# RWKV recurrence output: the v and u products merged over 128 rows, k-r taken apart from k-a

## What is computed

```python
def rwkv7_step(S, inp):
    r, w, k, v, a, b = inp
    sa = jnp.einsum('dbhvk,dbhk->dbhv', S, a)
    S = S * w[..., None, :] + sa[..., None] * b[..., None, :] + v[..., :, None] * k[..., None, :]
    y = jnp.einsum('dbhvk,dbhk->dbhv', S, r)
    return S, y
```

## Time and profile before

| what | value |
| --- | --- |
| median of 3 runs | 3094.26 us (3088.29 to 3096.70) |
| profiled execution | 3099.59 us, its span 3097.8 us, mean granted clock 0.955 |
| PE | busy 2801.7 us, 90% of the span |
| PE weight loads | busy 2233.2 us, 72% |
| DVE | busy 2077.6 us, 67% |
| ACT | busy 1340.7 us, 43% |
| POOL | busy 745.1 us, 24% |

### The profile page before, as it was taken

One profiled execution on the slowest core, in us unless ns is written; L12 is line 12 of the kernel. 1 busy time (PEld: TensorE's weight loads), 2 busy tenths in 40 slices (PEclk: granted clock), 3 DMA queues, 4 the chain that ended last, 5 costly groups with the idle time before them and its releaser, 6 DMA issues. The chain is left out here.

```text
span 3097.8 us, 62311 instructions
## 1 busy us (share of the span) xinstructions
PE 2801.7 (90%) x24610; PEld 2233.2 (72%) x24610; DVE 2077.6 (67%) x3080; ACT 1340.7 (43%) x2582; POOL 745.1 (24%) x895
## 2 busy tenths in 40 slices
PE   7889989997747999997899789999799999799999
PEld 4565578884447998895666678888588888588887
DVE  5767623236756665543545878888888888588786
ACT  4547711114434554443334434444544444344443
POOL 4547700004636787741223100000000000000000
PEclk9999999998868999998999899999899999899999
DMA  4432223224784444333555232222122222636411
GB/s 129 143 92 50 50 79 73 70 54 138 298 246 147 139 143 138 107 109 124 163 181 181 79 123 83 81 82 82 55 81 80 79 80 73 249 118 211 162 36 55
DMA packets 302490, 361.25 MB, mean 117 GB/s; under 512 B 119977, under 2 KB 202409, under 8 KB 302082
## 3 DMA queue, kind: packets, MB, share of 16 engines
q1 hardware_dynamic: 297314, 352.01, 35.6%
q10 hardware_dynamic: 4896, 5.38, 0.5%
HBM read 254.16 MB, written 103.14 MB: 115 GB/s over the span
## 5 line engine op out<-in xcount | busy, mean ns | idle before, releaser
L99 PE MATMUL up_p<-up_b_hi,up_a_hi 128*128 128x512 f32 x1232 | 491.1, 399 | 43.3 <-ACT inv L2286 23.3
L100 PE MATMUL up_p<-up_b_lo,up_a_hi 128*128 128x512 f32 x1232 | 490.8, 398 | 0.0
L101 PE MATMUL up_p<-up_b_hi,up_a_lo 128*128 128x512 f32 x1232 | 490.1, 398 | 0.0
L99 PEld LDWEIGHTS up_p<-up_b_hi,up_a_hi 128*128 128x128 f32 x1232 | 234.0, 190 | 104.3 <-ACT inv L2286 25.0
L100 PEld LDWEIGHTS up_p<-up_b_lo,up_a_hi 128*128 128x128 f32 x1232 | 234.0, 190 | 56.0
L101 PEld LDWEIGHTS up_p<-up_b_hi,up_a_lo 128*128 128x128 f32 x1232 | 233.9, 190 | 55.6
L2729 ACT CAST down_a_hi<-down_a 128x512 fp32r<-128x512 f32 x154 | 96.0, 623 | 260.6 <-PE down_p_x L101 144.6
L2241 ACT CAST up_a_hi<-up_a_sum 128x512 fp32r<-128x512 f32 x132 | 81.3, 616 | 231.7 <-DVE up_a_sum L2400 151.4
L2744 DVE TENSOR_TENSOR down_a_lo<-down_a,down_a_hi 128x512 fp32r<-128x512 f32 x154 | 106.4, 691 | 98.5 <-ACT down_a_hi L2729 98.5
L2311 ACT ACTIVATE up_con<-up_raw,vecs_sb 128x1023 f32<-128x1023 f32 (+1 forms) x88 | 109.7, 1246 | 127.7 <-DVE up_raw L2470 84.2
L99 PE MATMUL down_p_x<-down_b_hi,down_a_hi 128*128 128x512 f32 x352 | 138.8, 394 | 20.0 <-DVE down_b_lo L2746 19.9
(11 more groups left out here) (298 smaller groups left out, 7449.7 us busy)
## 6 DMA issues: line engine op xcount, KB each, us to landing
up_a_raw<-in_w_up SPq DMA_DIRECT2D x172, 256.0 KB, 2.9
rec_inp<-gate_chunks SPq DMA_DIRECT2D x64, 512.0 KB, 3.6
down_a<-in_w_down SPq DMA_DIRECT2D x88, 256.0 KB, 8.6
down_b<-act_out SPq DMA_DIRECT2D x88, 256.0 KB, 8.8
first_w<-in_w_attn SPq DMA_DIRECT2D x24, 512.0 KB, 3.6
rkv_chunks<-rwkv_project_mix SPq DMA_DIRECT2D x12, 1024.0 KB, 6.5
gate_chunks<-gates_out SPq DMA_DIRECT2D x3, 4096.0 KB, 13.4
act_out<-up_con SPq DMA_DIRECT2D x22, 512.5 KB, 2.6
```

Source lines behind the costliest of these rows:

```text
L99: pe.matmul(out, w_hi, x_hi, start=start, stop=False, skip_group_check=True)
L100: pe.matmul(out, w_hi, x_lo, start=False, stop=False, skip_group_check=True)
L101: return pe.matmul(out, w_lo, x_hi, start=False, stop=stop, skip_group_check=True)
```

## The change

`akrk` (64 rows of a head: masked k-a beside masked k-r) becomes `ak` alone; `rb` becomes `rbrk`, which for each head h holds the masked b-r product in the head's own 64 rows and the masked k-r product in the other 64 rows, the same layout as `stacked`. The y stage then multiplies `stacked` by `rbrk` over all 128 rows, one matmul for each head in place of two. To bring k-r into the opposite half, it is taken out of `ak_part` into a stage of its own, `rk_part`, which writes the half opposite to the rows that it reads, as `tok_part` does. `rk_part` takes the place of `rb_part` in PE's list, and `rb_part` goes behind `h_part`, with a wait for `rk` of its direction. The ak mask covers 64 columns, the rb mask now covers rb and rk together.

```diff
@@ -1102,7 +1102,7 @@
                   "kept_odd",
                   "dec", "grow", "g_copied", "x_copied", "u_copied", "m_copied", "tok_copied", "v_copied", "y_copied",
                   "spread", "ar", "diag_a", "diag_b", "ak_masked", "rb_masked", "h_added", "h_decayed",
-                  "merged", "b", "k", "gram", "cross", "corner", "x", "u", "h", "ak", "rb", "tok_b", "tok", "y", "v"):
+                  "merged", "b", "k", "gram", "cross", "corner", "x", "u", "h", "ak", "rk", "rb", "tok_b", "tok", "y", "v"):
             S[n] = [ctx.enter_context(nc.semaphore(f"rec_{n}{d}")) for d in range(2)]
         G = {n: ctx.enter_context(nc.semaphore("rec_" + n)) for n in
              ("init", "dec_set", "mask_in", "turned", "solved", "returned", "step", "eye_zero", "eye_set", "first_quarter_in")}
@@ -1116,8 +1116,8 @@
         kt = sb("k", RING, RU, L)
         dec_end = sb("dec_end", NCH, RU)
         ring_g = sb("g", RING, RU, L)
-        akrk = sb("akrk", 2, RU, 2 * L)
-        rb = sb("rb", 2, RU, L)
+        ak = sb("ak", 2, RU, L)
+        rbrk = sb("rbrk", 2, RU, 2, L)
         toks = sb("toks", RU, 2, L)
         raw_v = lambda d, r: toks[d][:, :, r % 2]
         vtok = sb("vtok", 2, RU, L)
@@ -1305,7 +1305,7 @@
                     for u in range(RU):
                         if c > 0:
                             pair(to[:, u], ar[d][:, c % RING, u, 0:L], H[d][:, c % 2, u], True, False)
-                        mm = pair(to[:, u], akrk[d][:, c % 2, u, 0:L], vtok[d][:, c % 2, u], c == 0, True)
+                        mm = pair(to[:, u], ak[d][:, c % 2, u], vtok[d][:, c % 2, u], c == 0, True)
                     mm.then_inc(S["x"][d], 1)
 
                 def u_part(c, d):
@@ -1329,24 +1329,36 @@
                     done(pe, "u_copied", d, c + 1)
                     to = bank[d][1][:, :, 0:L]
                     for u in range(RU):
-                        pair(to[:, u], vtok[d][:, c % 2, u], akrk[d][:, c % 2, u, L:], True, False)
                         if c > 0:
-                            pair(to[:, u], H[d][:, c % 2, u], ar[d][:, c % RING, u, L:], False, False)
+                            pair(to[:, u], H[d][:, c % 2, u], ar[d][:, c % RING, u, L:], True, False)
                         for h, rows in enumerate(HALVES):
-                            mm = pe.matmul(to[rows, u], stacked[d][rows, c % 2, u, h], rb[d][rows, c % 2, u],
-                                           start=False, stop=True)
+                            mm = pe.matmul(to[rows, u], stacked[d][:, c % 2, u, h], rbrk[d][:, c % 2, u, h],
+                                           start=c == 0, stop=True)
                     mm.then_inc(S["y"][d], 1)
 
                 def ak_part(c, d):
                     done(pe, "ar", d, c + 1)
                     done(pe, "k", d, c + 1)
                     done(pe, "g_copied", d, min(NCH, c + LAG - 1))
-                    each(bank[d][2], kt[d][:, c % RING], ar[d][:, c % RING]).then_inc(S["ak"][d], 1)
+                    each(bank[d][2][:, :, 0:L], kt[d][:, c % RING], ar[d][:, c % RING, :, 0:L]).then_inc(S["ak"][d], 1)
+
+                def rk_part(c, d):
+                    done(pe, "ak_masked", d, c + 1)
+                    to = bank[d][2].rearrange("p u (j t) -> p u j t", j=2)
+                    for u in range(RU):
+                        for h, rows in enumerate(HALVES):
+                            mm = pe.matmul(to[HALVES[1 - h], u, h], kt[d][rows, c % RING, u],
+                                           ar[d][rows, c % RING, u, L:], start=True, stop=True)
+                    mm.then_inc(S["rk"][d], 1)
 
                 def rb_part(c, d):
-                    done(pe, "ak_masked", d, c + 1)
-                    each(bank[d][2][:, :, 0:L], bt[d][:, c % RING], ar[d][:, c % RING, :, L:]).then_inc(
-                        S["rb"][d], 1)
+                    done(pe, "rk", d, c + 1)
+                    to = bank[d][2].rearrange("p u (j t) -> p u j t", j=2)
+                    for u in range(RU):
+                        for h, rows in enumerate(HALVES):
+                            mm = pe.matmul(to[rows, u, h], bt[d][rows, c % RING, u], ar[d][rows, c % RING, u, L:],
+                                           start=True, stop=True)
+                    mm.then_inc(S["rb"][d], 1)
 
                 def tok_b_part(c, d):
                     done(pe, "v_copied", d, NCH // 2)
@@ -1405,7 +1417,8 @@
                 for c in SLOTS:
                     now, ahead, front = live(c), live(c + 1), live(c + LAG)
                     for go, stage, n in ((now, x_part, c), (ahead, ak_part, c + 1), (now, u_part, c),
-                                         (ahead, rb_part, c + 1), (now and c < NCH - 1, h_part, c),
+                                         (ahead, rk_part, c + 1), (now and c < NCH - 1, h_part, c),
+                                         (ahead, rb_part, c + 1),
                                          (now, y_part, c), (ahead, tok_b_part, c + 1), (ahead, tok_part, c + 1),
                                          (ahead, cross, c + 1), (front, gram, c + LAG),
                                          (ahead, corner, c + 1)):
@@ -1550,13 +1563,15 @@
                 def ak_mask(c, d):
                     done(dve, "ak", d, c + 1)
                     done(dve, "y", d, c - 1)
-                    tt(akrk[d][:, c % 2], bank[d][2][:, :, :], over_units(mask_of(f"both{d}")), ALU.mult).then_inc(
-                        S["ak_masked"][d], 1)
+                    tt(ak[d][:, c % 2], bank[d][2][:, :, 0:L], over_units(mask_of(f"both{d}")[:, 0:L]),
+                       ALU.mult).then_inc(S["ak_masked"][d], 1)
 
                 def rb_mask(c, d):
                     done(dve, "rb", d, c + 1)
                     done(dve, "y", d, c - 1)
-                    tt(rb[d][:, c % 2], bank[d][2][:, :, 0:L], over_units(mask_of(f"both{d}")[:, L:]),
+                    tt(rbrk[d][:, c % 2].rearrange("p u j t -> p (u j) t"),
+                       bank[d][2].rearrange("p u (j t) -> p (u j) t", j=2),
+                       mask_of(f"both{d}")[:, L:].unsqueeze(1).to_broadcast([P, 2 * RU, L]),
                        ALU.mult).then_inc(S["rb_masked"][d], 1)
 
                 def state(c, d):
```

## The result

The changed kernel takes 3129.99 us (median of 4 runs, 3127.40 to 3135.60) against 3095.48 us of the kernel before in the same comparison: ratio 1.0107, 95% interval 1.0086 to 1.0128. It is slower by 34.5 us, inside the range, with the sign of the forecast; the forecast itself had +50.

A forecast was written before the change was run, and what follows sets the result against it. The prediction took PE's own stream to bound the recurrence, about 15.1 us a slot. Its terms, 44.0 - 0.6 + 3.8 + 3, summed to +50 us, giving 3144 us, with a range of 3112 to 3168.

The forecast's parts named there:

- What bounds it: Recurrence, 960 to 1430 us: PE's own stream sets its length, about 15.1 us a slot; PE idle under issue 23.3 us.
- The y stage, +44.0 - 0.6: Y stage: eight groups fewer, 16 changes of shape at 0.147 us; +1.42 us a slot over 31 chunks, chunk 0 -0.6.
- the second rival: Y stage, half the cost: second pair's weight load runs ahead, 0.09 us a change stays; +22 us, 3116 us; chance 0.10.
- the first rival: Y stage: no cost for changes of shape in short groups; -14 us, 3080, with 8 given back at y copies; chance 0.09.
- k-a and k-r apart, +3.8: Ak and rk stages: 64 columns each in place of 128 together, +0.12 us a slot, x 32 = +3.8 us.
- The ak mask, +3: PE reaches rk 0.82 us earlier and waits for DVE's ak mask: 7 us at most, taken as +3 us.
- The order on DVE, 0: Rb mask before the state update on DVE: state, x and block transposes move later but stay covered; cost 0.
- Issue pauses unchanged: PE's issue pauses in the recurrence, 23.3 us: no term in the sum; range allowed 10 us less or more.
- the third rival: Recurrence: issue pauses grow with the waits, or the broken-up y stage lowers the clock, 45 us on top; 3190; chance 0.04.
- The sum: Whole kernel: 44.0 - 0.6 + 3.8 + 3 = +50 us, +1.6%, giving 3144 us.
- the full cost: Main case, every change of shape in the y stage costs 0.147 us: range 3128 to 3160, chance 0.77.

The follow-up runs named there:

- experiment 4: Kernel before, with its h stage taken unit by unit into the y stage: 434 more changes of shape, nothing merged; 3134.25 us, ratio 1.0084.
- 1: Changed kernel without the merged product: k-r apart but written to its own half, y again in three groups; 3139.04 us, ratio 1.0102 to the kernel before.
- 6: Kernel before, with the 128-column ak product taken as two of 64, 992 matmul instructions more; 3123.62 us, ratio 1.0072.
- 2: Changed kernel, y stage in two passes for each direction, all H products first, then the merged ones; 3117.98 us, ratio 1.0035 to the kernel before.
- 3: Changed kernel, H products as a stage of their own between k-r and b-r, y one merged pass; 3119.75 us, ratio 1.004 to the kernel before.
- the repeats: Kernel before and changed kernel, unedited, profiled once more: 3109.97 us (one execution) and 3141.07 us (ratio 1.0109).
- 7: Against the kernel before: merged, k-a and k-r kept together, b-r, u and b's tokens in the opposite half, H products separate; 3094.20 us, ratio 0.9976.
- 11: The fewer-products merged kernel, with DVE transposing the solved blocks ahead of the b-r masks; 3086.63 us, ratio 0.9934 to the kernel before.

## Why the prediction was right, and where it wasn't

- **What bounds it.** Right: the time before and behind the recurrence moved by 2 us at most in the profile, the recurrence by 30.9. "PE's own stream sets the length" was true, but I took "issue" for a fixed remainder of that stream, and it is a second bound with a rate of its own.
- **The y stage, +44.0 - 0.6.** Right. The groups stand 0.264 us apart (mean of 440) against 0.265, and 98% of the 544 changes take 148 to 152 ns from the last start to the next, in place of 51 or 52 inside a stage; the second pair starts 107 ns behind the first, in place of 58. So the 0.147 has the parts 0.10 and 0.05, where the prediction, rounding, read 0.09 and 0.05. y, tok_b and rb, whose borders these are, grew by 30.6 + 4.8 + 3.1 = 38.5 us between the two u starts; my sum for the 30 full slots and chunk 0 there is 30 x 1.42 - 0.6 = 42. The step that rested on a choice, that the price seen once after 32 instructions holds every four, was right; experiment 4 shows it without a merged product. (The Trainium skill, "TensorEngine Tiling", Key Properties, has the drain and no price; the measured one is 0.14 to 0.147 us.) The second pair behind a change is late in short groups as well, so half the cost, the second rival, is out, and so is the first, for the price itself; the 3116 us of the second rival are 14 us from the measured median, no farther than my 3144, so it is the trace and not the time that tells them apart.
- **k-a and k-r apart, +3.8.** Right for the stream: ak, rk and u together went from 82.6 to 86.2 us. Wrong as the price of the step: done alone (1) it costs 32 us, because there it brings 32 more instructions a slot, their blocks (6: 19 us in the time from the instructions alone), and waits. In the changed kernel the merge takes these 32 away again. So the sum held and two of its terms did not stand for themselves: 1 at +32 and the merge on top of it at about 0, where I had +7 and +43.
- **The ak mask, +3.** The right mechanism, mis-sized: waits for `rec_akrk` were 1.1 us, for `rec_ak` 6.8, +5.7 from start to start, inside my 0 to 7.
- **The order on DVE, 0.** Right: waits for the spread went from 2.6 to 2.3 us, and x doesn't wait for the state. It is a cover that the long y stage gives. Where y is short again (2, 3) the waits for the spread are 11.6 and 13.3 us, 9 and 11 more than before, the case that the first rival had put at 8.
- **Issue pauses unchanged.** This is the step that failed, and nearly the whole error of the profiled sum: 31.4 to 14.6 us, -16.8 (in the repeats 38.8 to 26.2, -12.6). My text had them growing in the third rival and shrinking by 10 at most in the range. Longer slots with the same number of instructions give each block of them more time. The falling clock of the same rival hardly counts: it is 0.5 for 13.7 us where before had 6.8, by the distances between starts 1 to 2 us of the base.
- **The sum.** Base +42.5 (forecast 47.2), waits +5.2 (3), pauses -16.8 (0): +30.9 against +50. 3144 was 14 us too high. The measured 3130 is inside the range of the full cost, 3128 to 3160, but close to its lower end: the fall of the pauses alone was larger than the 10 us that this range allowed for, so that the time is still inside it owes something to luck. The slot is 500.4 / 31 = 16.1 us and not 16.7, for the same reason; PE's busy time grew with the stretch (441.8 to 483.1 us), and the waits for masks stay under 10 us, as written.

Open: why the time before the first u product differs by up to 22 us between profiles, and why single issue pauses last 3 us and more.

## What to carry to other kernels

Merging two products into one is worth nothing when the new product has another shape on the array than its neighbours: count the changes of shape, at 0.147 us each here against 0.117 for a group of four, and gather products of one shape into passes before merging any. On a stream of very short float32 products, also count instructions, because their blocks come at a rate of their own: idle time under "issue" at even distances in the count of instructions is a bound, which grows when PE gets denser and shrinks when it gets slower, so time saved on PE arrives only in part. Behind a wait of PE also look at the granted clock: where it falls to 0.5, the matmuls take longer, and that time stands in the trace as busy, not as idle. To get a merge's gain, choose the operand to move such that no product is added (7, 11: k-a and k-r stay together, and existing products change their half), then give the masks their time.

## What the runs showed of the hardware

- PE's instructions come in packets of 16 KB, 125 matmul instructions with their weight loads (109 packets for some 13650). PE resumes about 1.4 us after the end of a late one; in the profile of before the blocks ahead of a pause were used up in 3.7 us on average, the others in 4.1 us.
- Those pauses follow the data traffic: 31 to 39 us in the recurrence at 124 or 125 GB/s, 10.7 us at 81 GB/s, with the same instructions.
- 992 more matmul instructions of the shortest kind cost 19 us of the kernel's time and 11 to 15 in the recurrence, 4 to 7 of that as stream.
- Changes between 64\*64 and 128\*64 cost nearly the same in both directions: 148 ns to the next start when going to 128\*64, 152 ns back, in place of 51 or 52, and 107 ns to the second pair in place of 58.
- Behind some waits and pauses of PE the granted clock is at 0.5: for 6.8 us of the recurrence before, for 37.5 us in 3 and in 7. Matmul instructions start 53 ns apart there, 29 to 30 in the rest (3, 7).
